# Last two experts interleaved as up, up, down, down in a one-core mixture-of-experts layer, with one of the four closing squares on VectorE

## The reference

```python
D_MODEL = D_FF = 1024; SEQ = 256; N_EXPERTS = 32; TOP_K = 4
def clamped_swiglu(h):
    g = jnp.minimum(h[..., 0::2], SWIGLU_LIMIT)
    u = jnp.clip(h[..., 1::2], -SWIGLU_LIMIT, SWIGLU_LIMIT)
    return g * jax.nn.sigmoid(SWIGLU_ALPHA * g) * (u + 1.0)
...
    def expert_block(args):                      # rows of the tokens that chose expert e
        xb, e = args
        a = clamped_swiglu(xb @ w_up[e] + b_up[e])      # w_up[e]: 1024 x 2048
        return a @ w_down[e] + b_down[e]                # w_down[e]: 1024 x 1024
    yrows = lax.map(expert_block, (xrows, blk_e)).reshape(P, D)
    contrib = yrows[dest] * sw[:, None].astype(yrows.dtype)
    return jax.ops.segment_sum(contrib, stok, num_segments=N).reshape(B, S, D)
...
        x = x + moe_ffn(rmsnorm(x, ffn_norm_g[l]), ...)
    return rmsnorm(x, final_norm_g)              # x * rsqrt(mean(x*x) + 1e-5) * g
```

## Time and profile before

| | |
|---|---|
| median of 3 runs | 1076.32 us (1074.85 to 1077.40) |
| profiled execution: its own time, its span | 1077.45 us, 1075.4 us |
| PE busy | 1031.2 us (96%) |
| DVE, ACT, POOL busy | 223.5 us, 155.0 us, 20.0 us |
| moved by DMA | 423.35 MB, mean 394 GB/s |
| granted TensorE clock, mean | 0.995 |

### The profile page before, as it was taken

The page is one execution under the profiler, slowest core; times in us unless marked ns, Lnnn a source line. Parts: engine busy times, 40 slices in busy tenths (PEclk is TensorE's granted clock), DMA queues, the critical chain, the costliest instruction groups (busy, mean ns, idle before and its releaser), DMA issues.

```text
span 1075.4 us, 12842 instructions
## 1 busy us (share of the span) xinstructions
PE 1031.2 (96%) x5122; PEld 411.5 (38%) x5122; DVE 223.5 (21%) x633; ACT 155.0 (14%) x389; POOL 20.0 (2%) x49
## 2 busy tenths in 40 slices
PE   8999999999999999999999999999999999999996
PEld 6776663333333333333333333333333333333332
DVE  3354533111111111111111111111112101111112
ACT  1233431111100110001111111111101100011102
POOL 4011000000000000000000000000000000000000
PEclk8999999999999999999999999999999999999999
DMA  9993378999999999999999999999999999999994
GB/s 283 317 351 129 121 288 356 403 399 428 427 428 431 433 432 433 431 428 430 431 431 433 435 431 430 430 431 431 436 429 433 430 429 427 427 427 427 428 425 193
DMA packets 36972, 423.35 MB, mean 394 GB/s; under 512 B 8242, under 2 KB 12386, under 8 KB 19012
## 3 DMA queue, kind: packets, MB, share of 16 engines
q1 hardware_dynamic: 36688, 422.34, 94.1%
q10 hardware_dynamic: 244, 0.42, 0.1%
HBM read 421.70 MB, written 1.05 MB: 393 GB/s over the span
## 4 chain that ended last, share of the span: by engine, by line
PE 77%; DMA 19%; DVE 3%; ACT 1%; issue 0%; DVEq 0%; ACTq 0%; SPq 0%
PE ps L1163 31%; DMA ring<-in_w_up_dram 18%; PE ps L1196 17%; PE ps L1208 5%; PE ps L1118 4%; PE ps L941 4%; PE ps L1028 3%; PE ps L948 2%; PE ps L1143 2%; PE ps L979 1%; DVE work L1637 1%; PE ps L1133 1%; DVE work L1681 1%; PE ps L1176 1%; PE ps L1055 1%; PE ps L1067 1%
## 5 line engine op out<-in xcount | busy, mean ns | idle before, releaser
L1163 PE MATMUL ps<-ring,work 128*64 128x512 f32 x2040 | 447.4, 594 | 8.6 <-DMA ring<-in_w_up_dram 8.1
L1163 PEld LDWEIGHTS ps<-ring,work 128*64 128x64 f32 x2040 | 142.7, 137 | 310.3 <-issue 290.7
L1196 PE MATMUL ps<-ring,work 128*64 128x512 f32 x1008 | 223.3, 595 | 21.1 <-DVE work L1681 21.1
L1646 DVE TENSOR_SCALAR work<-ps 128x512 f32<-128x512 f32 x31 | 21.4, 692 | 642.9 <-PE ps L1163 642.9
L1196 PEld LDWEIGHTS ps<-ring,work 128*64 128x64 f32 x1008 | 69.8, 137 | 154.5 <-issue 129.0
L821 ACT ACTIVATE work<-work 128x512 f32<-128x512 f32 x31 | 19.5, 630 | 453.8 <-DVE work L1646 453.8
L1208 PE MATMUL ps<-work 64*128 64x512 f32 x256 | 63.6, 615 | 0.7 <-ACT work L833 0.7
L1118 PE MATMUL ps<-xt,work 128*64 128x512 f32 x256 | 60.6, 593 | 0.2 <-DVE work L1595 0.2
L833 ACT ACTIVATE work<-ps 128x512 f32<-128x512 f32 x32 | 19.1, 597 | 236.5 <-PE ps L1196 236.5
L941 PE MATMUL ps<-extra,ring 128*128 128x256 f32 x192 | 42.7, 380 | 0.0
L1208 PEld LDWEIGHTS ps<-work 64*128 64x128 f32 x256 | 22.0, 186 | 41.8 <-issue 40.2
(11 more groups left out here) (254 smaller groups left out, 525.7 us busy)
## 6 DMA issues: line engine op xcount, KB each, us to landing
ring<-in_w_up_dram SPq DMA_DIRECT2D x40, 4096.0 KB, 35.8
ring<-in_w_up_dram SPq DMA_DIRECT2D x43, 2048.0 KB, 18.2
ring<-in_w_down_dram SPq DMA_DIRECT2D x20, 4096.0 KB, 35.9
ring<-in_w_down_dram SPq DMA_DIRECT2D x21, 2048.0 KB, 15.6
ring<-in_w_up_dram SPq DMA_DIRECT2D x9, 1024.0 KB, 13.6
ring<-in_w_in_dram SPq DMA_DIRECT2D x8, 1024.0 KB, 9.4
ring<-in_w_out_dram SPq DMA_DIRECT2D x4, 1024.0 KB, 9.7
ring<-in_w_down_dram SPq DMA_DIRECT2D x4, 1024.0 KB, 30.0
```

The source lines that it names most:

```text
L1163: t = pe.matmul(UP[h * 64:h * 64 + 64, a, :], xgT[:, k, :], row[:, a * 64:(a + 1) * 64, h, :], start=False, stop=(k == KD - 1), skip_group ...
L1196: t = pe.matmul(ps[h * 64:(h + 1) * 64, XG, :], aT[:, j, u * 64:u * 64 + 64], w[:, j * D + h * 512:j * D + (h + 1) * 512], start=(u == 0 a ...
L1646: dve.tensor_scalar(t1, up_pairs[:, 0], 7.0, None, ALU.min).then_inc(swi, 1)
```

## The change

The two last experts are interleaved. Their twelve units are loaded and used in the order up(30), up(31), down(30), down(31) (`turn_of`). The transposes of expert 31's activations and combine weights stand between the two units of down(30); its combine weights are turned into bank XTB, and its down goes to bank XTB too, into buffers of its own (`aT_end` is t1, `cT_end` a part of t2). `combine(30)` stands between the two units of down(31). The last unit of all is loaded as a half of 1 MB and two rows of 0.5 MB; the up unit that was split into halves is whole again. The SwiGLU of the last expert is the ordinary one. At the end VectorE does the square of token tile 0, half 1: a copy out of PSUM, then `tensor_tensor_reduce`. Each half sum goes as a bias (`end_base`) into the root of the other (`end_root`). ScalarE itself issues the output DMAs of tile 0.

```diff
+        aT_end = t1
+        cT_end = t2[:, 0:2, :]
...
+        def turn_of(b, u):
+
+            if b < E - 2:
+                return EXPERT_UNITS * b + u
+            if u < UP_UNITS:
+                return EXPERT_UNITS * (E - 2) + UP_UNITS * (b - (E - 2)) + u
+            return EXPERT_UNITS * (E - 2) + 2 * UP_UNITS + DOWN_UNITS * (b - (E - 2)) + u - UP_UNITS
...
-                if b == E - 1 and u in last_half_in:
+                if (b, u) == (E - 1, EXPERT_UNITS - 1):
                     load_half(b, u, 0, half_of(single(g), 0), place_in[spot(g - 1)])
-                    load_half(b, u, 1, half_of(single(g), 1), last_half_in[u])
+                    for i in range(2):
+                        sp.dma_start(single(g)[:, (2 + i) * D:(3 + i) * D], down_v[b][:, (6 + i) * D:(7 + i) * D])\
+                          .then_inc(last_row_in[i], 16)
...
-            with act.Fori(TAIL, E - 1) as i:
+            with act.Fori(TAIL, E - 2) as i:
                 run(i)
-            act.wait_ge(last_swi, 1)
-            act.activation(t2[:, :, 0:64], t1[:, :, 0:64], ACT.Sigmoid, scale=1.702).then_inc(last_sig, 1)
-            act.wait_ge(swi, (E - 1) * 3 + 1)
-            act.activation(t2[:, :, 64:P], t1[:, :, 64:P], ACT.Sigmoid, scale=1.702).then_inc(sig_done, 1)
+            select(E - 1, E - 1)
+            sigmoid(E - 2)
+            read_xg(E - 1)
+            act.wait_ge(comb_done, E - 2)
+            read_cT(E - 2, cT, XG)
+            read_aT(E - 2, aT)
+            sigmoid(E - 1)
             act.activation(root[:, 5:6], ident[:, 0:1], ACT.Sqrt)
-            read_rest(E - 1, True)
+            read_aT(E - 1, aT_end)
+            read_cT(E - 1, cT_end, XTB)
+            read_y(E - 2)
+            act.wait_ge(down_used, E * DOWN_UNITS)
+            act.wait_ge(comb_done, E - 1)
+            act.activation(yv, ps[:, XTB, :], ACT.Copy).then_inc(y_read, 1)
...
+            def end_root(n, half, count):
+                act.wait_ge(squared[0], count)
+                act.wait_ge(base_ready, n + 1)
+                act.activation(root[:, 4 + n:5 + n], sq_sum[:, 4 + n, half:half + 1], ACT.Sqrt, scale=1.0 / D, bias=ms[:, 4 + n:5 + n])\
+                   .then_inc(rooted, 1)
+
+            square_sum(0, 0, end_dump[0])
+            square_sum(1, 0, dump[0])
+            end_root(0, 0, 7)
             square_sum(1, 1, dump[1])
-            take_root(5)
+            end_root(1, 1, 9)
             act.wait_ge(rstd_ready, 5)
             for half in range(2):
                 h = slice(512 * half, 512 * half + 512)
                 act.wait_ge(scaled_by_g, half + 1)
                 act.activation(xs[:, 0, h], xs[:, 0, h], ACT.Copy, scale=rstd[:, 4:5]).then_inc(fin_act, 1)
+                act.wait_ge(fin_act, half + 1)
+                act.dma_start(out_v[0][:, h], xs[:, 0, h]).then_inc(out_sent, 16)
...
+            def down_unit(b, u, w, acts, bank, last=False):
+
+                for j in range(4):
+                    if last and j >= 2:
+                        pe.wait_ge(last_row_in[j - 2], 16)
+                    for h in range(2):
+                        t = pe.matmul(ps[h * 64:(h + 1) * 64, bank, :],
+                                      acts[:, j, u * 64:u * 64 + 64],
+                                      w[:, j * D + h * 512:j * D + (h + 1) * 512],
+                                      start=(u == 0 and j == 0), stop=(u == DOWN_UNITS - 1 and j == 3),
+                                      skip_group_check=True)
+                t.then_inc(down_used, 1)
...
+            def combine_end(b):
+
+                pe.wait_ge(y_read, b + 1)
+                for n in range(NT):
+                    for h in range(2):
+                        pe.matmul(ps[:, OUT[n][h], :], cT_end[h * 64:(h + 1) * 64, n, :], yv[h * 64:(h + 1) * 64, :],
+                                  start=False, stop=True, skip_group_check=True)\
+                          .then_inc(half_summed if (n, h) != (1, 1) else comb_done, 1)
...
+            for b in range(TAIL, E - 2):
                 table_read = tables(b)
                 if b == TAIL + 1:
                     down_bias()
                 if b == TAIL + 3:
                     residual()
                 run(b, in_pairs((b - SINGLES) // CYCLE, (b - SINGLES) % CYCLE) if b < LATE else in_singles(b), table_read)
-            last = in_singles(E - 1)
-            up(E - 1, True, last, last=True)
+            unit, last = in_singles(E - 2), in_singles(E - 1)
+            up(E - 2, True, unit)
+            gather(E - 1)
+            combine(E - 3)
+            combine_turn(E - 2, 1)
+            gather_turn(E - 1)
+            act_turn(E - 2)
+            up(E - 1, True, last)
+            pe.wait_ge(aT_read, E * 2 - 2)
+            pe.wait_ge(cT_read, E - 1)
+            down_unit(E - 2, 0, unit(UP_UNITS), aT, XG)
+            act_turn(E - 1)
+            combine_turn(E - 1, 0, XTB)
+            down_unit(E - 2, 1, unit(UP_UNITS + 1), aT, XG)
+            pe.wait_ge(aT_read, E * 2)
+            pe.wait_ge(cT_read, E)
+            down_unit(E - 1, 0, last(UP_UNITS), aT_end, XTB)
             combine(E - 2)
-            combine_turn(E - 1, 0)
-            act_turn(E - 1)
-            down(E - 1, last, last=True)
-            combine(E - 1, last=True)
+            down_unit(E - 1, 1, last(UP_UNITS + 1), aT_end, XTB, last=True)
+            combine_end(E - 1)
...
-            swiglu_last(E - 1)
-            read_aT(E - 1)
+            swiglu(E - 1)
+            read_aT(E - 1, aT_end)
...
+            def end_base(n, half):
+                dve.tensor_scalar(ms[:, 4 + n:5 + n], sq_sum[:, 4 + n, half:half + 1], 1.0 / D, EPS, ALU.mult, ALU.add)\
+                   .then_inc(base_ready, 1)
+
             def scale_by_g(half):
                 h = slice(512 * half, 512 * half + 512)
-                dve.wait_ge(squared[0], 7 + half)
                 dve.tensor_tensor(xs[:, 0, h], total(0, half), gfin[:, h], ALU.mult).then_inc(scaled_by_g, 1)
 
             def finish(half):
@@ -1796,11 +1828,19 @@
                                          in1=gfin[:, h], op0=ALU.mult, op1=ALU.mult).then_inc(fin_dve, 1)
 
             dve.wait_ge(gfin_in, 16)
+            dve.wait_ge(half_summed, 2)
+            dve.tensor_copy(end_dump[1], total(0, 1)).then_inc(squared[1], 1)
+            dve.wait_ge(squared[1], 2)
+            dve.tensor_tensor_reduce(xs[:, 0, 512:1024], total(0, 1), end_dump[1], 1.0, 0.0, ALU.mult, ALU.add,
+                                     sq_sum[:, 4, 1:2]).then_inc(squared[1], 1)
+            dve.wait_ge(squared[1], 3)
+            end_base(0, 1)
+            dve.wait_ge(squared[0], 7)
             scale_by_g(0)
-            mean(4, ((0, 8),))
+            dve.wait_ge(squared[0], 8)
+            end_base(1, 0)
             scale_by_g(1)
             invert(4)
-            mean(5, ((0, 10),))
             invert(5)
             finish(0)
```

More of the change, by code:

```diff
@@ L258, in hybrid_layer @@
         pair_in = [sem(f"pair_in{u}") for u in range(PAIRS)]
-        last_half_in = {u: sem(f"last_half_in{u}") for u in (3, 5)}
+        last_row_in = [sem(f"last_row_in{i}") for i in range(2)]
         g_in = sem("g_in")
@@ L402, in job_bank @@
             return ps[:, PJ[job_at[name] % 2], :]
+        def turn_of(b, u):
[4 more added lines that the diff above has]
+            return EXPERT_UNITS * (E - 2) + 2 * UP_UNITS + DOWN_UNITS * (b - (E - 2)) + u - UP_UNITS
+        unit_of = {turn_of(b, u): (b, u) for b in range(E) for u in range(EXPERT_UNITS)}
         def single(g):
@@ L821, in sigmoid, with read_cT, read_aT, read_y @@
                 act.activation(t2, t1, ACT.Sigmoid, scale=1.702).then_inc(sig_done, 1)
+            def read_cT(b, into, bank):
+                act.wait_ge(cT_done, b + 1)
+                act.activation(into, ps[:, bank, 0:256].rearrange("p (n q) -> p n q", n=2), ACT.Copy).then_inc(cT_read, 1)
+            def read_aT(b, into):
+                act.wait_ge(aT_done, b + 1)
+                act.activation(into[:, 0:2, :], UP[:, 0, 0:256].rearrange("p (a q) -> p a q", a=2), ACT.Copy)\
+                   .then_inc(aT_read, 1)
+            def read_y(b):
+                act.wait_ge(down_used, b * DOWN_UNITS + DOWN_UNITS)
+                act.activation(yv, ps[:, XG, :], ACT.Copy).then_inc(y_read, 1)
             def read_rest(b, prev):
-                act.wait_ge(cT_done, b + 1)
                 if prev:
                     act.wait_ge(comb_done, b)
[L828 to L833, removed]
+                read_cT(b, cT, XG)
+                read_aT(b, aT)
+                read_y(b)
             def select(b, e):
@@ L1146, in up_bias, with up @@
                 t.then_inc(bias_used, 1)
-            def up(b, prev, unit, biased=False, last=False, halves=False):
+            def up(b, prev, unit, biased=False, halves=False):
                 if not biased:
@@ L1184, in act_turn, with down @@
                 t.then_inc(aT_done, 1)
-            def down(b, unit, last=False):
```

(25 more changed lines are left out.)

54 lines of the change are left out of this document (10 added, 44 removed).

## The result

| | before | after |
|---|---|---|
| median, first comparison (9 runs each) | 1075.38 us (1074.63 to 1077.40) | 1078.26 us (1077.08 to 1079.17) |
| ratio after / before | | 1.0023 (95%: 1.0014 to 1.0032) |
| ratio, second comparison (11 runs) | | 1.0016 (1.0007 to 1.0025) |
| profiled execution, span | 1077.45, 1075.4 us | 1078.80, 1076.8 us |

The change makes the kernel slower, by 1.35 us between the two profiled executions (1077.45 and 1078.80) and by 1.7 to 2.5 us in the two ratios. The forecast was 1.16 us slower, 1077.5. One execution of 1821.01 us at a granted clock of 0.555, of the old order without its waits for data, was in a slow state and stands in no ratio here.

The account below looks back on a forecast made before the run. The end was taken as TensorE's, with the DMA 1 us behind. The later last combine (+1.24) and the tail (-0.08) gave +1.16 us, a median of 1076.32 becoming 1077.5; range 1075.2 to 1079.0.

Parts of the forecast that it names:

- The loads come no earlier: DMA queue: transfers 184 to 191 start and land as before, only with other contents; reordering costs SP nothing.
- Down unit by down unit: TensorE after up(31): waits 0.2, 0.7 and 1.4 us for transfers 188, 189, 190; down(31) ends 1.24 us later.
- A shorter list of work, longer waits: TensorE since 1032.34: 1.1 us of waits around transposes and in up gone, 2.3 us of data waits added.
- Rival 1: Loads 188 to 190 land before they are wanted, so the end is 1.05 us earlier: 1075.2; chance 0.19.
- SwiGLU(31) hidden under down(30): Done at 1050.4 under down(30)'s unit 0, hiding the 0.5 us TensorE waited before down(31).
- The tail: After the last combine starts: first root at +2.9 us as before, last issue +6.3 against +6.36, 0.1 gained.
- the term of -0.08 in the sum: Tail's part of the sum, beside +1.24 for the later last combine, giving +1.16 us.
- Rival 2: Outputs issued by ScalarE land last, 4.0 us after issue instead of 2.8: +1.2 us, 1078.7; chance 0.15.
- Rows of half a megabyte: Last megabyte's two rows take 1.2 us each, at the halves' pace; no effect on the sum.
- The size: Whole kernel: +1.24 - 0.08 = +1.16 us; from a median of 1076.32 to 1077.5, leaning to slower.
- Within 0.2%: Outcome not told from no change, 0.2% being 2.15 us; chance 0.72, slower 0.21, faster 0.07.

Follow-up runs that it names:

- the old order without its waits for data: Kernel before with transfer 187 cut from 4096 to 64 columns, so later transfers land nearly one unit earlier; ratio to before 0.9995 (0.9984 to 1.0006).
- the new order without waits: Changed kernel with transfer 187 cut from 4096 to 64 columns, so later transfers land nearly one unit earlier; ratio to before 0.9992 (0.9983 to 1.0001).
- S: Trace stretch, not a run: TensorE's first record on transfer 188 to the last combine's start; 18.30 us before, 19.64 after.
- four moves: Changed kernel with units 189 and 190 in halves, expert 31's transposes behind down(30), combine(30) before down(31), y(30) copied first; ratio to before 0.9997.

## Why the prediction was right

- **The loads come no earlier.** Right: 190 lands at 1057.22 after and at 1057.4 before.
- **Down unit by down unit.** The waits were put at 0.2, 0.7 and 1.4; those shown are 0.27, 0.34 and 1.33. The second is smaller in the row because TensorE's last record on the transposes ends only at 1052.03 by the model; the unit's start, 1052.37, lies 0.13 before the 1052.5 worked out. The last combine was forecast at 1067.14 and starts at 1067.21.
- **A shorter list of work, longer waits.** Right, and shown by taking the waits away: 0.76 us shorter without them, 1.3 longer with them. Rival 1 is what the change would do if the loads were one unit ahead: it put the end 1.05 earlier, and the new order without waits is 33.56 - 32.43 = 1.13 shorter than before with its own.
- **SwiGLU(31) hidden under down(30).** Right: it runs from 1047.34 to 1050.08 and the transposes start at 1051.15 without a wait.
- **The tail.** Its operations came within 0.15 us: `tensor_tensor_reduce` at 512 columns takes 0.69, the value chosen between 0.42 and 0.84, and the first root is at +2.97 against +2.9. The gain of 0.1 from the last issue did not come: the term of -0.08 in the sum measured +0.03. That step took the last issue for what the end waits for; by the rows the end waits for 1 MB to flow, which begins with the first issue. Rival 2 rested on the same idea and fell with it: an output issued by ScalarE lands after 2.1 to 3.0 us, as SP's do (2.1 to 2.8 before).
- **Rows of half a megabyte.** Nothing, as taken: TensorE waits for neither row. The Trainium skill's rule to make DMAs of at least 1 MiB (DMA: Bandwidth & Descriptors, Measured), which the page draws from DMAs issued by GpSimd, would have had the pieces late; behind 40 us of queue they landed 1.3 us apart. That is no rate of transfer, as the last section shows.
- **The size.** 1.16 us was forecast, the traces show 1.40, the ratios 1.7 us (0.7 to 2.7) and 2.5 us (1.5 to 3.4). The forecast lies below the first comparison's interval and within the second's and that of the order alone. That the measured median, 1078.26, lies only 0.8 above the 1077.5 of the forecast is in part luck: the forecast stood on a median of 1076.32 from three executions, and nine gave 1075.38. "Within 0.2%" had most of the chance, and the first comparison came out just over it, the second just under. Whether half a microsecond or so beyond S and the tail is real is open: it would have to lie ahead of the last two experts, where both kernels issue the same work. The copy of aT(30) ends between 1029.90 and 1032.47 in the twelve traces, on average at 1030.90 in the five of the old order and 1031.41 in the seven of the new, less apart than the traces of either order are among themselves, so they don't show it.

## What to carry to other kernels

When loads and matmuls keep the same pace, as here, an order that shortens TensorE's list can lose, because what counts for each transfer is its landing plus all the work that still stands behind it; write that sum down for the last four or five transfers, and the largest is the end. Put ready work into each wait for data, and split a transfer so that its first rows can be used while the rest comes: with the same idea but four moves, 1.3 us lost became 0.8 gained between the same two points. An execution's scatter of 2 us can hide this, a stretch between two fixed points of the trace repeats to a few hundredths.

## What the runs showed that was not expected

- The tail doesn't follow its last issue. Three arrangements of it (+6.36, +6.17, +5.9 us) end 9.52, 9.55 and 9.48 us after the last combine began; what they share is the first issue at +5.0 and the flow of the four outputs.
- On VectorE a square read from PSUM costs two passes here, a copy of 0.69 and a product of 0.69, against one of 0.60 on ScalarE. Where each engine takes 0.6 to 0.7 for 512 columns, handing over one of four squares leaves the first root where it was.
- The wait for transfer 190 is no want of bandwidth. Here is the microsecond before it lands, in the kernel after, and the 1.3 us between the landings of the two rows, in the run of the rows alone (stretch and its length in us, busy us of each engine, then granted clock, mean busy share of the 16 DMA engines, GB/s):

```profile
1056.00:1057.00 1.00, 0.02 (x2) 0.00 (x0) 0.00 (x0) 0.60 (x1) 0.00 (x0) 1.00 0.50 205
...
1059.00:1060.30 1.30, 1.30 (x8) 0.43 (x6) 0.00 (x0) 0.00 (x0) 0.00 (x0) 1.00 0.12 47
```

All loads had been issued by then, so half of the DMA capacity had nothing left to move while TensorE waited, and nearly all of it between the rows. The packet records of the kernel after say the same: about 1055 the packets under way at one time fall from 16 to 8, and one of 4 KB takes 159 ns before and behind that fall. So a transfer lands when the engine that is last with its share has moved it, and the spacing of the landings is that engine's: 0.5 MB in 1.3 us would be 400 GB/s, where 47 were moved. Why some of the 16 fall behind was not looked for.
